# Router products of a mixture-of-experts layer: one column group replaced by four

## The reference

```
logit_g = (xt @ w_group + b_group).astype(F32)            # 512 x 4
g_sel   = jnp.argmax(logit_g, -1)
logit_e = (xt @ w_router + b_router).astype(F32)          # 512 x 16
logit_e = take the four of group g_sel
top_v, top_i = lax.top_k(jax.nn.softmax(logit_e, -1), 2)  # two experts per token
```

## Time and profile before

| what | value |
|---|---|
| median of 3 runs | 939.82 us (937.27 to 940.77) |
| profiled execution | 938.98 us |
| its span, first to last instruction | 937.2 us |
| PE busy | 911.9 us, 97% |
| DVE, ACT, POOL busy | 363.8, 217.7, 164.0 us |
| PE share of the chain that ended last | 89% |
| granted TensorE clock | 1.00 throughout |

### The profile page before, as it was taken

How to read it: one execution, slowest core, us unless ns; L and a number is a source line. 1 busy time by engine, 2 the same in 40 slices (tenths; PEclk the granted TensorE clock), 3 DMA queues, 4 the chain that set the end, 5 groups by cost and what they waited for, 6 DMA issues and landing times.

```text
span 937.2 us, 12906 instructions
## 1 busy us (share of the span) xinstructions
PE 911.9 (97%) x5308; PEld 505.7 (54%) x5308; DVE 363.8 (39%) x798; ACT 217.7 (23%) x474; POOL 164.0 (17%) x159
## 2 busy tenths in 40 slices
PE   7999999999999989999999999999999999999998
PEld 3588864445555443333334333334688888755543
DVE  2754432357674463210310210047535533444321
ACT  2211213344555200010010110123202111633310
POOL 3212220000002144050130100032202211430000
PEclk9999999999999999999999999999999999999999
DMA  9935559124010977999999999961482012500002
GB/s 327 302 108 180 180 180 380 46 90 180 1 46 0 305 169 266 396 406 427 425 417 428 421 427 429 402 222 45 116 195 92 23 45 62 208 1 1 1 12 78
DMA packets 71451, 188.43 MB, mean 201 GB/s; under 512 B 31184, under 2 KB 31840, under 8 KB 65120
## 3 DMA queue, kind: packets, MB, share of 16 engines
q1 hardware_dynamic: 62416, 162.41, 47.2%
q0 software_dynamic: 5488, 18.37, 5.4%
q10 hardware_dynamic: 3488, 6.82, 1.9%
HBM read 168.70 MB, written 18.89 MB: 200 GB/s over the span
## 4 chain that ended last, share of the span: by engine, by line
PE 89%; DVE 4%; DMA 2%; ACT 2%; issue 1%; POOL 1%; ACTq 0%; SPq 0%; DVEq 0%; POOLq 0%
PE psum L924 21%; PE psum L1118 18%; PE psum L1139 8%; PE psum L1269 6%; PE psum L1025 6%; PE psum L835 5%; PE psum L950 5%; PE psum L973 5%; PE psum L987 3%; PE psum L1004 2%; PE psum L1325 2%; PE psum L1231 1%; PE psum L1355 1%; PE psum L887 1%; PE psum L1052 1%
## 5 line engine op out<-in xcount | busy, mean ns | idle before, releaser
L1118 PE MATMUL psum<-ring,buf_a 128*32 128x512 f32 x1536 | 171.3, 593 | 3.5 <-issue 3.3
L1118 PEld LDWEIGHTS psum<-ring,buf_a 128*32 128x32 f32 x1536 | 60.0, 110 | 111.2 <-issue 111.2
L1139 PE MATMUL psum<-ring,buf_c 128*32 128x512 f32 x768 | 86.3, 593 | 0.2
L2569 POOL DMA_INDIRECT buf_b<-xq_d,o_sb x48 | 50.7, 1057 | 164.2 <-DVE buf_a L2187 132.8
L2210 DVE TENSOR_TENSOR buf_c<-buf_c,psum 128x512 f32<-128x512 f32 x12 | 13.1, 1089 | 158.9 <-PE psum L1118 158.9
L2496 POOL TENSOR_TENSOR qk_st<-qk_st,half 128x8 f32<-128x8 f32 x26 | 43.6, 1677 | 158.7 <-DVE qk_st L2268 71.4
L924 PE MATMUL psum<-ring,buf_a 128*128 128x256 f32 x320 | 71.3, 380 | 0.0
L924 PEld LDWEIGHTS psum<-ring,buf_a 128*128 128x128 f32 x320 | 60.0, 190 | 9.4 <-issue 1.7
L924 PE MATMUL psum<-ring,buf_b 128*128 128x256 f32 x288 | 64.9, 381 | 0.0
L1835 DVE TENSOR_TENSOR s_buf<-s_buf,psum 128x512 f32<-128x512 f32 x52 | 35.3, 685 | 63.9 <-PE psum L924 59.9
L1025 PE MATMUL psum<-ring,buf_b 128*128 128x512 f32 x128 | 59.8, 594 | 0.0
(11 more groups left out here) (307 smaller groups left out, 1155.7 us busy)
## 6 DMA issues: line engine op xcount, KB each, us to landing
ring<-in_moe_w_gate SPq DMA_DIRECT2D x16, 2048.0 KB
ring<-in_moe_w_up SPq DMA_DIRECT2D x16, 2048.0 KB, 14.8
ring<-in_moe_w_down SPq DMA_DIRECT2D x16, 2048.0 KB, 15.0
ring<-in_w_in SPq DMA_DIRECT2D x7, 2048.0 KB, 11.2
ring<-in_w_ada SPq DMA_DIRECT2D x6, 2048.0 KB, 9.7
ring<-in_da_w_in SPq DMA_DIRECT2D x5, 2048.0 KB, 20.8
y_d<-ring POOLq DMA_DIRECT2D x1, 5632.0 KB, 21.9
y_d<-buf_b ACTq DMA_DIRECT2D x11, 512.0 KB, 12.1
```

The lines of the kernel that those rows point to most:

```text
L1118: last = mm(buf("mm", n)[rows, :], x_part[:, j, k, :], slot(moe_load(q, m, r))[:, k, :], start=(k == 0), stop=(k == KD - 1))
L1139: last = mm(buf("sc", n)[rows, m, :], hidT[:, s % 3, f * P + SUB * j:f * P + SUB * (j + 1)], slot(moe_load(q, 2, r), FC)[:, f, m * CH:(m + ...
L2569: pool.indirect_dma_start(out=xg[:, s % 2, j * 256:(j + 1) * 256], out_offset=None, in_=xn_quarters, in_offset=bass.IndirectOffsetOnAxis(a ...
```

## The change

Router products now go to four groups of 32 PSUM partitions: product `k = 4r + j` goes to partitions 32j to 32j+31, with the weights padded by zeros from 20 to 32 columns. So each group holds the sum of two products, and the whole bank of 128 partitions is filled. ACT copies all 128 x 512. The four transposes become four products whose right side `rt_fold` is a matrix of 128 x 32 that has a 1 where the partition's number modulo 32 is the column's; so the product both turns the tile and adds the four groups.

The padded weights and `rt_fold` stand in `pd`, which is in use until the attention's last scores are transposed. So the multiplication by `norm_ffn` is moved from before the attention steps to the end of `norm2_first`, behind a wait for the last transpose of `pd`, and three DVE instructions stand there.

```
+    logit_parts = pT[:, 0, :]
+    w_rt_pad = pd[:, 0, 0:KD * 32].rearrange("p (k n) -> p k n", n=32)
+    rt_fold = pd[:, 0, KD * 32:KD * 32 + 32]
...
+        def router_parts(cols):
+            for r in range(2):
+                for j in range(4):
+                    k = 4 * r + j
+                    if cols.start == 0:
+                        drained(pe, "tp", turn["tp", "xT2", k])
+                    else:
+                        drained(pe, "tp", turn["tp", "xT2_last", r])
+                    last = mm(buf("mm", n_r)[32 * j:32 * j + 32, cols], w_rt_pad[:, k, :], xT2[:, k, cols],
+                              start=(r == 0), stop=(r == 1))
+            return last
...
-            mm(buf("mm", n_r)[0:20, 0:LAST], w_rt[:, k, :], xT2[:, k, 0:LAST], start=(k == 0), stop=(k == KD - 1))
+        router_parts(slice(0, LAST))
...
-            last = mm(buf("mm", n_r)[0:20, LAST:SEQ], w_rt[:, k, :], xT2[:, k, LAST:SEQ], start=(k == 0), stop=(k == KD - 1))
+        fill(router_parts(slice(LAST, SEQ)), "mm", n_r)
...
-            last = transpose(buf("mm", n)[:, t * 20:(t + 1) * 20], logit_T[:, t * P:(t + 1) * P], ident[0:20, 0:20])
+            last = mm(buf("mm", n)[:, t * 20:(t + 1) * 20], logit_parts[:, t * P:(t + 1) * P], rt_fold[:, 0:20],
+                      start=True, stop=True)
...
-        drain(S.copy(logit_T, buf("mm", n)[0:20, :]), "mm", n)
+        drain(S.copy(logit_parts, buf("mm", n)), "mm", n)
...
-        V.tensor_tensor(w_rt[:], w_rt[:], gain2[:].unsqueeze(2).to_broadcast([P, KD, 20]), ALU.mult).then_inc(w_rt_ready, 1)
...
                 elif name == "norm2_first":
                     norm2(range(TT - 2))
+                    filled(dve, "tp", turn["tp", "pdT", TT * HEADS - 1])
+                    V.tensor_reduce(rt_fold, ident[:].rearrange("p (j b) -> p b j", b=32), AX.X, ALU.add)
+                    link(V.memset(w_rt_pad, 0.0))
+                    V.tensor_tensor(w_rt_pad[:, :, 0:20], w_rt[:], gain2[:].unsqueeze(2).to_broadcast([P, KD, 20]),
+                                    ALU.mult).then_inc(w_rt_ready, 1)
```

More of the change, by code:

```diff
@@ L320, in build @@
     sel = sel_pad[:, TT:2 * TT, :]
-    logit_T = pT[0:20, 0, :]
+    logit_parts = pT[:, 0, :]
+    w_rt_pad = pd[:, 0, 0:KD * 32].rearrange("p (k n) -> p k n", n=32)
+    rt_fold = pd[:, 0, KD * 32:KD * 32 + 32]
     last_pick = o_sb[:, 0:512]
@@ L1059, in _ @@
         claim(pe, "mm", n_r)
-        for k in range(KD):
-            drained(pe, "tp", turn["tp", "xT2", k])
-            mm(buf("mm", n_r)[0:20, 0:LAST], w_rt[:, k, :], xT2[:, k, 0:LAST], start=(k == 0), stop=(k == KD - 1))
+        router_parts(slice(0, LAST))
         pe.wait_ge(xs2_ready, TT)
@@ L1067, in _ @@
             transposes(n, [xs2[:, TT - 1, k * P:(k + 1) * P] for k in range(4 * b, 4 * b + 4)])
-        for k in range(KD):
-            drained(pe, "tp", turn["tp", "xT2_last", k // 4])
-            last = mm(buf("mm", n_r)[0:20, LAST:SEQ], w_rt[:, k, :], xT2[:, k, LAST:SEQ], start=(k == 0), stop=(k == KD - 1))
-        fill(last, "mm", n_r)
+        fill(router_parts(slice(LAST, SEQ)), "mm", n_r)
         n = turn["mm", "router"]
```

## The result

| | kernel before | changed kernel |
|---|---|---|
| median of 20 runs | 938.33 us (935.76 to 941.37) | 941.78 us (936.41 to 951.97) |
| ratio, without the run of 951.97 us | 1 | 1.0028, 95% interval 1.0015 to 1.0042 |
| profiled execution, span | 938.98, 937.2 us | 945.65, 943.9 us |
| granted TensorE clock, that execution | 1.000 | 0.987 |
| mean granted clock of the runs | 0.9973 (128 runs beside the experiments) | 0.9924 (19, without the one of 951.97 us) |

Forecast were 939.5 us and a range of 937.4 to 941.5. The medians differ by 3.4 us, and that of the changed kernel lies just above the range. One run, of 951.97 us, is over 1.5% above the fastest and is left out of the ratio; by the ratio the change costs 2.6 us (1.4 to 3.9). That is within 0.5%, but a loss where a gain was forecast, and the interval excludes zero.

The account below looks back on a forecast made before the run. PE, busy for 97% of the span, was taken as the bound, with the router on its path. Transposes -0.10, last products -0.93, copy +0.02, turning +0.72 gave about -0.3 us: median 939.5 us, range 937.4 to 941.5.

Parts of the forecast that it names:

- Step 1: Three new DVE instructions at the end of `norm2_first`: 0.9 us on DVE, PE 0.85 us later from 305.19 on.
- Step 2: Router products of 384 tokens: at most 1.92 us instead of 5.27; PE then idle over 2 us, 0.10 us gained.
- D: Rival: DVE's delay decides, a loss if over 1.2 us; at 1.6 us +0.4, 940.2 us; chance 0.16.
- The sign that I had named for being wrong: First expert products over 1 us away from 346.1, or first gather waiting for the copies' stores, not the row numbers.
- Step 3: Last tile's router products in groups: second half 0.47 us after DVE's copy, gain 0.93 us.
- Step 4: ACT's copy of the logits, 128 partitions instead of 20: +0.02 us, 0.1 at worst.
- Step 5: Turning the logits by four products instead of four transposes: 1.27 us from the copy's end against 0.53, taken as +0.72.
- not a new bound, but near: Before the gather: copies land in DRAM at 337.45, 0.85 us later than before, 0.17 us ahead of the row numbers.
- B: Rival: DVE's new work is hidden, transposes begin 0.95 us earlier; -1.1 us, 938.7 us; chance 0.12.
- C: Rival: the groups' full gain at the router counts; -3.6 us, 936.2 us; chance 0.04.
- E: Rival: grouped products run one behind another, first ones still 5.27 us; +1.6 us, 941.4 us; chance 0.03.
- A: The forecast itself: DVE's delay reaches PE, logits slightly earlier; -0.3 us, 939.5 us; chance 0.62.

Follow-up runs that it names:

- e5: Kernel before with only the change's three DVE instructions, in the changed kernel's place; products and turning as before: 938.38 us, ratio 0.9999.
- e1: Changed kernel with three thrown-away products on PE in its idle time before the last tile's transposes: 939.35 us, ratio 1.0006.
- e2: Kernel before with four thrown-away DVE products ahead of the last tile's normalization, so that PE idles there: 943.55 us, ratio 1.0056.
- e3: Changed kernel with the three new DVE instructions moved behind `gate_diag`; PE's idle time stays: 940.51 us, ratio 1.0015.
- e4: Changed kernel, but only the last tile in four groups, three turnings as transposes, DVE's instructions behind `gate_diag`: 937.93 us, ratio 0.9997.
- e13: Changed kernel with e10's thrown-away products at the expert products only; idle time at the router stays: 943.23 us, ratio 1.0048.
- e7: Kernel before with the 12 stores of tiles 0 to 2 issued earlier, behind the weight load of `i == 2`: 937.70 us, ratio 0.9979.
- e10: Kernel before with two thrown-away products before the first set of expert products and three before the second: 936.78 us, ratio 0.9983.
- e12: e4 with the 12 stores issued earlier and e10's thrown-away products at the expert products: 937.74 us, ratio 0.9987.
- e16: e4 with e10's thrown-away products at the expert products, stores not moved: 940.42 us, ratio 1.0017.
- e9: Changed kernel with one thrown-away product instead of e1's three in PE's idle time at the router: 939.97 us, ratio 1.0019.
- e6: e1 with the 12 stores of tiles 0 to 2 issued behind the weight load of `i == 2`: 939.07 us, ratio 1.0005.
- e8: Changed kernel with DVE's new work late, three thrown-away products at the router and the 12 stores issued earlier: 936.94 us, ratio 0.9976.
- e11: e8 with e10's thrown-away products at the expert products: 939.56 us, ratio 1.0027.
- e14: Changed kernel with e1's thrown-away products at the router and e10's at the expert products: 948.45 us, ratio 1.0113.
- e15: e14 with DVE's new work moved late, off the path, no store moved: 943.77 us, ratio 1.0067.

## Why the prediction was wrong

**What bounds the kernel.** Right: PE waits where the first products stood. What this part lacks is the question what the clock does when PE's share falls in one stretch. The share of the whole execution couldn't tell: it is 97% in both kernels. The Trainium skill ("TensorE: Matmul & The Clock Gate", "What's actually happening") says that a gate on the clock follows how busy PE has been, with 1.2 and 2.4 GHz as its levels. The windows above show both levels, 1.00 and 0.50, and the lower one behind PE's idle time; the rule should have been a rival.

**Step 1, DVE's work: right.** Forecast 0.9 us, measured 0.92; the MEMSET took 0.27 us, not 0.33, the reduction 0.38, not 0.36. The 0.27 us is what the Trainium skill's rule of one cycle per element ("VectorE: DVE Perf Modes") gave. At PE the delay is 0.69 us at tile 2, where I had 0.85. e5 shows 0.71 us at PE. The last transposes start 0.24 us earlier than before (320.07 - 0.26 against 320.05), where I had 0.10.

**Step 2, first products: this is the step that failed.** Its sizes were right. 16 instructions took 1.50 us (I had at most 1.92) and PE "stands idle for more than 2 us", in fact 2.79. I priced this idle time at nothing, booked 0.10 us of gain, and took every length behind it at full clock. The clock was 1.00 until PE went on, then fell to 0.50 and stayed there for some 10 us. e1 has the same steps without the idle time: no fall, 3.43 us less up to the row numbers. e2 has the idle time without the change: it falls. e3 has the idle time (2.78 us) without DVE's delay: it falls. e4 has neither: it doesn't, and its time is that of before. Over all 18 profiles: the four with 2.6 to 2.8 us of idle time at the router (changed kernel, e2, e3, e13) all fall behind it; the seven others where the 384 tokens are multiplied in one group (kernel before, e4, e5, e7, e10, e12, e16; no idle time over 0.80 us there) don't from 310 to 335 us, nor does e9 with 1.73 us; of the six filled ones four (e1, e6, e8, e11) don't and two (e14, e15) do, for 3 to 4 us. What brings those two falls is open. In the list of rivals none was the clock. D's price, +0.4 us, hung on a delay over 1.2 us, and it was 0.92; e3 and e5 show that the delay isn't what makes the clock fall. The sign that I had named for being wrong did come: the first expert products start at 349.61, 3.5 us from 346.1.

**Step 3, last products: right where the clock is full.** Forecast 0.47 us for the second half, measured 0.47 in e1 and e4; in the changed kernel 0.70, at half clock.

**Step 4, the copy: right.** 0.59 us, forecast 0.60.

**Step 5, the turning: right at full clock.** 1.15 us forecast, 1.04 in e1; 1.86 in the changed kernel.

**The sum, and the stores.** The terms behind the transposes are -0.25 us in e1 against -0.19 forecast. The second thing I called "not a new bound, but near", the landing of the copies, is a bound in part: where the clock holds, the gather waits for it, 2.74 us beyond the usual 0.85 in e1's profile, 0.35 in e5's, 0.54 in e6's. In the changed kernel it doesn't show, because the row numbers are later still. The term that was off is the time of the last store: I let it move by the delay of 0.85 us, but it starts at 336.2 in the changed kernel and 335.4 in e1 and e5, before at 333.2, so 2.2 to 3.0 us later. The queue takes 18.66 us for its 16 stores in the kernel before and 20.67, 20.16 and 20.50 in those three; the third store alone takes 6.79, and 8.66 in the changed kernel. DVE's delay isn't enough to do this, since e9 has it and its last store starts at 333.2. This may be why e1, with the router's 3.4 us back, was only 2.4 us faster than the changed kernel (a difference across two sets of runs, and less sure than the ratios).

**Rivals.** B is out: the delay shows in full at L2038. C is out: PE waited. E is out: 1.50 us, not 5.27. A's terms for the router held one by one; 939.5 is at the upper end of the changed kernel's four runs at 0.996 and 0.998 (936.41 to 939.59 us).

**Open.** Why one store holds its queue for 5 to 9 us and the last one goes out later in some versions than in others; what makes the clock fall for 3 to 4 us where no idle time over 0.80 us is near (e14, e15, e12, and the changed kernel at 341 us); why the first expert set is broken by gaps on one chip (and in the kernel before's own profile, where a first piece has only 50 of the 64 instructions) and not on others; and how much of the 3.4 us in the medians are the other falls, at the expert products above all. The first fall is shown in the profiles; that it makes most of the loss in the medians rests on the runs' mean clocks and on e1 and e4.

## What to carry to other kernels

Before work on PE is made shorter, look at what PE does next: if it then waits, the time won is idle, and idle time can cost more than its length, since the clock may drop for what follows. Do the dense form where its end is on the path (the last tile) and leave the slow form where PE would only wait; or put useful work there. Here the dense form in that place won no more than the noise (e4, 0.9997). And look at the queue that carries what the next stage waits for: moving part of its work ahead can push the rest back (e6). And read the granted clock window by window, in runs of both kernels: a loss that hides in every instruction at once has no line of its own.

## What was not expected of the hardware

- The granted clock fell after an idle time of 2.79 us, and was back only some 10 us later, though PE was busy for 8.94 of the 10 us from 320 to 330. In e3 and e13, too, it fell for some 10 us, in e2, after 2.63 us of idle time, for 3 to 4 us: 0.84 and 0.81 in the two windows.
- It also fell, for 3 to 4 us, where PE's last idle times were 0.59 us (changed kernel at 341 us, e12 at 337 us) or 0.80 us (e14, e15 at 324 us), while e1, with the same idle times of 0.24 and 0.80 us, kept it.
- Sixteen stores of 128 KB, issued one behind another on one queue, took 18.5 to 20.7 us to issue: most 0.70 us, one of them 6.4 (e5) to 8.7 us (changed kernel).
- The kernel before isn't free of it either. Its profiled execution has a clock of 1.000, but of the 128 runs beside the experiments only 11 have that, ten of them on one chip; 75 have 0.998 and 31 have 0.996, with medians of 937.87 and 939.32 us. The one profiled execution did not show this.
- Over 19 of the 20 runs of one kernel the time follows the mean clock nearly on a line, 0.8 us for each 0.001.
- Groups of 32 columns: 16 instructions of 384 columns ended within 1.43 to 1.50 us, eight of 128 columns within 0.47, at full clock; changing between them and full-width products showed no price of its own.
